# Experts' first weights: one 512-column product for parts and rests, VectorE adds the halves, rests beside the gates on GpSimd

## The reference, cut to what matters

```python
q = (xt @ w_query).reshape(T, H, 2, PEER_HALF)
s = jnp.einsum('thcd,cnd->thcn', q, sub_keys)
sv, si = lax.top_k(s, K)                      # 16 best of 128, two halves, 8 heads
cand_s = (sv[:, :, 0, :, None] + sv[:, :, 1, None, :]).reshape(T, H, K * K)
top_s, pos = lax.top_k(cand_s, K)             # 16 best of the 256 sums
gate = jax.nn.softmax(top_s, axis=-1)
a = jnp.einsum('thkd,td->thk', down[ib], xb)  # experts' first weights
c = gb * jax.nn.gelu(a)
out = jnp.einsum('thk,thkd->td', c, up[ib])   # experts' second weights
```

## Time and profile before

| | us |
|---|---|
| median of 3 runs (2509.37 to 2515.11) | 2512.91 |
| the profiled execution: its own time | 2512.55 |
| its span, first to last instruction | 2510.7 |
| PE busy | 2432.4 (97%) |
| DVE busy | 1623.3 (65%) |
| ACT busy | 1206.1 (48%) |
| POOL busy | 697.0 (28%) |

### The profile page before, as it was taken

One profiled execution on the slowest core, in us unless ns is written; L12 is line 12 of the kernel. 1 busy time (PEld: TensorE's weight loads), 2 busy tenths in 40 slices (PEclk: granted clock), 3 DMA queues, 4 the chain that ended last, 5 costly groups with the idle time before them and its releaser, 6 DMA issues.

```text
span 2510.7 us, 40330 instructions
## 1 busy us (share of the span) xinstructions
PE 2432.4 (97%) x16355; PEld 2228.2 (89%) x16355; DVE 1623.3 (65%) x3095; ACT 1206.1 (48%) x1827; POOL 697.0 (28%) x333
## 2 busy tenths in 40 slices
PE   4999898999999999999999999999999999999999
PEld 3997888988889999999888888899999999888887
DVE  6887776546575676899544445664676899644444
ACT  4443675445554444443444445655445443444443
POOL 3111001112125661000344443115663000244443
PEclk9999999999999999999999999999999999999999
DMA  7888444655345554444566655435555444555655
GB/s 278 322 303 323 150 140 152 218 193 181 110 146 176 177 178 158 143 137 142 193 195 192 197 190 195 133 129 179 177 173 171 137 141 143 178 196 191 197 191 164
DMA packets 126588, 457.45 MB, mean 182 GB/s; under 512 B 13973, under 2 KB 16961, under 8 KB 125634
## 3 DMA queue, kind: packets, MB, share of 16 engines
q1 hardware_dynamic: 121442, 441.52, 53.1%
q10 hardware_dynamic: 4048, 8.91, 1.1%
q0 software_dynamic: 912, 4.42, 0.5%
...
## 4 chain that ended last, share of the span: by engine, by line
PE 83%; DVE 2%; ACT 1%; issue 0%; POOL 0%; ACTq 0%; POOLq 0%
PE bank L608 25%; PE bank L609 25%; PE bank L610 25%; PE bank L1176 4%; PE bank L956 1%; PE bank L1147 1%; PE bank L817 1%; DVE sb L1852 0%; PE bank L1099 0%; PE bank L623 0%; PE bank L974 0%; POOL sb L2743 0%; DVE sb L1905 0%; PE bank L806 0%; PE bank L1061 0%
## 5 line engine op out<-in xcount | busy, mean ns | idle before, releaser
L608 PE MATMUL bank<-sb,sb 128*128 128x256 f32 (+1 forms) x4744 | 1520.5, 321 | 36.5 <-DVE sb L1852 23.7
L609 PE MATMUL bank<-sb,sb 128*128 128x256 f32 (+1 forms) x4744 | 1494.0, 315 | 0.0
L610 PE MATMUL bank<-sb,sb 128*128 128x256 f32 (+1 forms) x4744 | 1493.9, 315 | 0.0
L1219 ACT ACTIVATE sb<-sb 128x1024 fp32r<-128x1024 f32 x765 | 808.1, 1060 | 1085.2 <-PE bank L610 1077.2
L1852 DVE TENSOR_TENSOR sb<-sb,sb 128x1024 fp32r<-128x1024 f32 x509 | 625.2, 1229 | 585.1 <-ACT sb L1219 583.8
L608 PEld LDWEIGHTS bank<-sb,sb 128*128 128x128 f32 x4744 | 907.9, 191 | 104.6 <-issue 20.9
L2720 POOL TENSOR_TENSOR sb<-sb,sb 128x1024 fp32r<-128x1024 f32 x256 | 629.3, 2460 | 1336.6 <-ACT sb L1219 1332.6
L609 PEld LDWEIGHTS bank<-sb,sb 128*128 128x128 f32 x4744 | 908.9, 192 | 55.0 <-issue 1.0
L610 PEld LDWEIGHTS bank<-sb,sb 128*128 128x128 f32 x4744 | 907.8, 191 | 55.9
L2684 DVE TENSOR_TENSOR sb<-sb,sb 128x1024 fp32r<-128x1024 f32 x64 | 159.9, 2498 | 149.8 <-ACT sb L1808 149.8
L2647 DVE TENSOR_SCALAR sb<-sb,sb 128x128 f32<-128x128 f32 x512 | 142.5, 345 | 0.0
...
## 6 DMA issues: line engine op xcount, KB each, us to landing
sb<-in_peer_down_dram SPq DMA_DIRECT2D x256, 512.0 KB, 3.3
sb<-in_peer_up_dram SPq DMA_DIRECT2D x256, 512.0 KB, 3.3
...
```

What stands on the lines that cost most here:

```text
L608: e.matmul(out, a[0], b[0], start=start, stop=False)
L609: e.matmul(out, a[0], b[1], start=False, stop=False)
L610: return e.matmul(out, a[1], b[0], start=False, stop=stop)
L1219: self.e.activation(rr(M.hi[k % NSPLIT]), M.raw[k % NRAW], AF.Copy).then_inc(*self.S.tick("hi", k))
```

## The change

A `down` tile is now multiplied by `linear_wide`: `hhi` and `hlo` of a chunk lie so that one matmul with the rounded weights streams both, 512 columns into a whole bank; a second one adds the rest of the weights times `hhi` to the first 256 columns. That is 16 matmuls in place of 24, with the same columns in all. The bank then holds two halves that belong together, one tile in a bank. VectorE adds them (`add_halves`, one reduction over pairs for each tile, 512 elements in and 256 out, from PSUM into `temp`), and ScalarE takes GELU from `temp`; where a product with gates follows, GELU goes back into the first bank of the pair, and VectorE's product (`put`) of pair n stands one tile after that pair's sums. VectorE makes all rests of the gates' stretch no longer: they go to GpSimd. `iota` is put into a PSUM bank by one matmul, held for the whole stretch, and compared from there.

```diff
-    "peer": ((1, ("dve",)), (3, ("pool",)), (11, ("dve", "pool")), (73, ("pool", "pool", "pool", "dve")), (137, ("dve",)),
+    "peer": ((1, ("dve",)), (3, ("pool",)), (11, ("dve", "pool")), (73, ("pool", "pool", "pool", "dve")), (137, ("pool",)),
...
+    def linear_wide(self, bank):
+        M, e, k = self.M, self.e, self.taken()
+        hi, lo = self.weights(k)
+        self.after_low(k)
+        for c in range(8):
+            self.wait_ge("h_lo", self.s, "x", c)
+            w = slice(128 * c, 128 * (c + 1))
+            e.matmul(bank, hi[:, w], rr(M.h[:, :, c]), start=(c == 0), stop=False)
+            x = e.matmul(bank[:, 0:256], lo[:, w], rr(M.hhi[:, c]), start=False, stop=(c == 7))
+        x.then_inc(*self.S.tick("tile", k))
+        self.used()
+
+    def down(self, n):
+        s, banks = self.s, []
+        for i in range(2):
+            bank = self.take()
+            self.K.bank["down", s, n + i] = bank
+            banks.append(bank)
+            self.linear_wide(bank)
+        self.give(banks[0], ("gelu_put", s, n) if self.gate_counts(n) >= 8 else ("down_sum", s, n))
+        self.give(banks[1], ("down_sum", s, n + 1))
...
@@ Tensor.search
-            self.give(bank, ("chosen", s, t, 1))
             for _ in range(17):
                 yield
+            self.give(bank, ("chosen", s, t, 1))
@@ Tensor.gates
+        bank = self.take()
+        self.K.bank["iota", self.s] = bank
+        self.e.matmul(bank[:, 0:128], self.M.const("ident"), self.M.const("iota"), start=True, stop=True).then_inc(
+            *self.S.tick("iota", self.s))
...
+        self.give(bank, ("one_hot1", self.s, 63))
@@ Tensor.peer
-            self.pair(("down", s, n), [("gelu", s, n)])
+            self.down(n)
@@ Scalar.put
-        src = self.K.bank["down", s, n].rearrange("p (n t) -> p n t", n=2)
+        src, gated = m.temp, self.K.bank["down", s, n].rearrange("p (n t) -> p n t", n=2)
-        self.wait_ge("tile", self.i - 1)
+        self.wait_ge("down_sum", s, n + 1)
...
-            if n > 72:
-                self.wait_ge("gelu_put", s, n - 2)
-            x = e.activation(m.temp[:, :, 0:done], src[:, :, 0:done], AF.Gelu_apprx_tanh)
+            x = e.activation(gated[:, :, 0:done], src[:, :, 0:done], AF.Gelu_apprx_tanh)
@@ Vector.gates
-        iota, wide = M.const("iota").unsqueeze(1).to_broadcast([128, 4, 128]), [128, 4, 128]
+        self.wait_ge("iota", s)
+        row = self.K.bank["iota", s][:, 0:128]
+        iota, wide = row.unsqueeze(1).to_broadcast([128, 4, 128]), [128, 4, 128]
...
-                x = e.tensor_scalar(o1[:, j], M.const("iota"), m.keep[:, 1, t:t + 1], m.keep[:, 0, t:t + 1], op0=ALU.is_equal,
+                x = e.tensor_scalar(o1[:, j], row, m.keep[:, 1, t:t + 1], m.keep[:, 0, t:t + 1], op0=ALU.is_equal,
...
+    def add_halves(self, n):
+        m, s = self.m, self.s
+        if n:
+            self.wait_ge("gelu", s, n - 2)
+        for i in range(2):
+            self.wait_ge("tile", self.i - 2 + i)
+            self.e.tensor_reduce(m.temp[:, i], self.K.bank["down", s, n + i].rearrange("p (u t) -> p t u", u=2), AX.X, ALU.add).then_inc(
+                *self.S.tick("down_sum", s, n + i))
...
@@ Vector.peer
-            self.linear(2)
-            self.put(n)
+            self.linear()
+            if n and n <= 124:
+                self.put(n - 2)
+            self.linear()
+            self.add_halves(n)
+            if n >= 124:
+                self.put(n)
```

More of the change, by code:

```diff
@@ L2678, in put @@
             self.wait_ge("gelu", s, n)
[L2679 removed]
+            src = self.K.bank["down", s, n].rearrange("p (n t) -> p n t", n=2)[:, :, 0:done]
+            self.e.tensor_tensor(dst, src, dst, ALU.mult).then_inc(*self.S.tick("gelu_put", s, n))
     def up(self, n):
```

4 lines of the change are left out of this document (2 added, 2 removed).

## The result

The changed kernel takes 2553.58 us, median of 4 runs (2552.98 to 2555.44), beside 2512.8 us for the kernel before on the same chip: a ratio of 1.0165, 95% interval 1.0147 to 1.0182. It is slower by 41 us. The profiled execution has a span of 2551.6 us, 40.9 over that of before.

What follows compares the result with a forecast made beforehand. PE's own stream was taken as the bound in the stages the change touches. 2512.55 - 27.3 (stream) + 0.4 (`iota`) + 32 + 20 (search waits) + 2 (gates) - 0.4 (last gates' products) = 2539.3, say 2539 us; range 2509 to 2566.

Steps and rivals of the forecast that it cites:

- PE's stream, 0.107 a tile: `down` tiles on PE: a tile takes 2.773 us in place of 2.88, -27.3 us for 256 tiles in both stages.
- waits of the search: Tiles 0 to 61: PE waits behind VectorE's sums, GELU, `hi` and GpSimd's rest; +32 and +20 us, both stages.
- beside the gates, with `iota`: Tiles 62 to 125: VectorE slightly late in the last blocks, +1 us a stage; `iota` matmuls +0.4 for both.
- the last two `down` tiles: PE's idle 0.4 us before the last gates' products may go, since one-hot rows come earlier: -0.4 us.
- rival D: GpSimd hinders comparisons from PSUM beside the gates, 60 us; or 512 columns from two places stream slower, 2566 us; chance 0.06.
- The ten tiles named: Search tiles 11, 15, 19, 23, 27, 35, 39, 47, 51, 55 of a stage: PE idles 1 to 3 us each.
- what is brought along: Search: VectorE's lateness from earlier pairs and rests colliding with GpSimd's, 10 us a stage, +20 for both.
- a lump of 6 us a stage: Search: VectorE's rests start later while a GpSimd rest runs, about six places, some 6 us a stage.
- Rival C: Search: PE's clock falls to 0.50 behind waits, 14 x 1.7 = 24 us more, 2563 us; chance 0.16.
- Rival A: Search: VectorE works well ahead, sums come in time, only PE's saving counts: 2485 us; chance 0.13.
- Rival B: Search: waits are there but small, with a sum of 0.34 us in place of 0.68: 2513 us; chance 0.10.

Runs made afterwards that it cites:

- e3_together: The changed kernel with parts and rests of a chunk side by side, so a matmul's 512 columns are one piece of memory: 2551.88 us.
- e1: The changed kernel, but in the search ScalarE takes GELU of a pair one tile later, behind the next tile's `hi`: 2518.78 us.
- e2: The changed kernel, but in the search VectorE takes a pair's sums before the search step of its second tile: 2530.51 us.
- e4: The changed kernel, but all rests of tiles 11 to 72 of a stage come from GpSimd, none from VectorE: 2502.34 us.
- e12_filler: The changed kernel with six more products of 512 columns on PE ahead of seven waiting `down` tiles, filling idle time: 2549.44 us.
- e7_wide_first: The changed kernel, but a `down` tile begins with its eight 512-column products, which need only `hi`: 2546.07 us.
- e8_all: The changed kernel with GpSimd's rests in tiles 11 to 72, 512-column products first, and the gates' copy ahead of GELU: 2489.95 us.

## Why the prediction was right, and where it was not

The forecast was 2539 us, range 2509 to 2566, slower with 0.74. It is 2554: the sign and the mechanism were right, and the time is 14.6 us above the forecast. By its own steps, each for both stages, in us:

| step | forecast | measured |
|---|---|---|
| PE's stream, 0.107 a tile | -27.3 | -20.3 |
| waits of the search | +52 | +55.3 |
| beside the gates, with `iota` | +2.4 | +2.4 |
| the last two `down` tiles | -0.4 | +3.4 |
| `up` tiles | 0 | +1.1 |
| all else | 0 | -1.0 |
| sum | +26.7 | +40.9 |

**PE's stream was mis-sized.** 0.107 a tile stood on two rates taken from places where matmuls of one width follow each other, 0.2267 and 0.120. Where the widths alternate there are two rhythms, and only one gives that sum. Against it the stream takes 3.9 us more in the searches and 3.1 beside the gates, mostly in the tiles at 2.83 and 3.71: 7 us of 27.3. It is not the layout (e3_together), which the second half of rival D had named. What sets the rhythm stays open.

**The waits were right in place and in sum.** The ten tiles named, and the eleventh (25), are the ones that wait, released by GpSimd's rest, behind GELU, behind the sums. e1, e2 and e4 each cut that chain at another link, and took 34, 29 and 53 of the 55 us. In the parts it was less exact. Without the low clock (e12_filler) 50.0 us are waits. There the tiles whose step is a head (11, 35, 39) wait 1.1 to 1.4 us for 1.16 forecast; the seven of 1.58 to 1.85 wait 2.2 to 2.9 (at tile 55, where 1.2 more were forecast for what is brought along, 2.5 for 3.0); tile 25 waits 2.1 for 2.6, and tile 59, which was not named, 0.9. Most of the extra goes with VectorE's rest being held up by GpSimd's: in the searches of that kernel it takes up to 2.5 us in place of 1.2. The prediction had this in a lump of 6 us a stage. So the sum, 52 forecast and 50.0 without the low clock, is closer than its parts, and that much of it is luck. What it did not have is that the wait is a loop (e7_wide_first): VectorE's next pair depends on `hi`, that on GELU, that on the sums of this pair. It reckoned each tile from PE's end. In this kernel both ways give nearly the same number (1.85 and what GpSimd holds up, against 2.5 a round of the loop), and only the experiments tell them apart.

**Rival C**, the fall of the clock, came about in mechanism: seven times in the two searches the granted clock fell to 0.50 behind a wait, for 3.4 us (once 6.8). Its price was wrong. It was 1.7 us for each of fourteen waits, 24 in all; half as many brought it, and it is 4 to 5 in all (e12_filler), most of the half-speed work falling into time in which PE would have been idle.

**Rival A** (VectorE well ahead) fell with the reason given against it: the rest can't come ahead of `hi`. It is the kernel that e4_rests_pool makes, 2502 us where rival A said 2485, and e8_all reaches 2490. **Rival B** fell with the reduction: 686 ns mean, as taken from the row of 512 elements from SBUF (676), not half of it. (Its 10 us for 0.6 at ten places of both stages should have been 12; nothing hangs on that.)

**Beside the gates** the forecast held: 0.406 us for a comparison from PSUM, 1.36 for four, so 0.32 apart for 0.33 taken, and of the 2.4 us some 0.5 are the `iota` matmuls and 1.9 the longer tiles 120, 122 and 124. The term that failed is the last one, -0.4. VectorE, up to 0.5 us a pair behind in the last blocks, was called covered by two buffers, and the idle time before the last gates' products was to go. The buffers did not cover it: in the last pairs VectorE takes 7.57 us a pair where PE wants 7.35, and PE waits 1.83 us at tile 126, which puts the last two tiles of both stages together 3.8 us off the forecast. The cause is a wait that the prediction had counted on VectorE (about 1.1 us in each pair for GELU and the copy) but not questioned; with the copy ahead of GELU it went.
